# A two-layer decoder trunk in float32 split products: the expert loop takes two experts per turn, with one gather of 256 columns for both

## The chip, the cores and the metric

One core of a Trainium2 chip runs the whole program in one launch. The metric is the device time of an execution in microseconds (us). The profile is of one execution, taken by the hardware profiler; its engines are PE (TensorE; PEld are its weight loads), DVE (VectorE), ACT (ScalarE), POOL (GpSimd) and SP (SyncE, which issues the transfers).

## The reference, cut to what matters

256 tokens of width 1024 go through two layers. Each has an attention and convolution part (not touched by the change), and then a channel mixer: dense in layer 0, top-2-of-8 experts in layer 1.

```python
def swiglu(h, w1, w3, w2):
    return (jax.nn.silu(h @ w1) * (h @ w3)) @ w2

def moe_swiglu(h, router, w1, w3, w2):
    logits = (h @ router).astype(jnp.float32)
    top_vals, top_idx = lax.top_k(logits, TOP_K)
    top_w = jax.nn.softmax(top_vals, axis=-1)
    combine = jnp.sum(jax.nn.one_hot(top_idx, N_EXPERTS) * top_w[..., None], axis=-2)
    y = jnp.zeros(h.shape, jnp.float32)
    for e in range(N_EXPERTS):
        y = y + combine[..., e:e + 1] * swiglu(h, w1[e], w3[e], w2[e])
    return y
```

w1 and w3 of an expert are 1024 x 3584, w2 is 3584 x 1024, all float32, so the eight experts hold 352 MB, read once each.

## The kernel before, in words

**Split products.** Weights come in pieces of 1 MB (128 x 2048 float32) into a ring of 7 (`raw(t)`, `RAW`). For each piece ACT casts the high part to fp32r (`high_part`, L458), DVE subtracts it to get the low part (`low_part`, L686), and PE multiplies three times: high x high, high x low, low x high (12 matmuls of 512 columns a piece in `up`, L1320 to L1322, and in `down`, L1342 to L1344). There are 3 pairs of buffers for split pieces (`SPLIT`), so ACT may cast piece t only when PE is through with piece t - 3 (`w_used`). SP issues piece t + 7 when the low part of piece t is made.

**The expert loop.** A turn `j` is one expert and one pass over at most 128 of its tokens; a count on the device sets the number of turns, 8 with these inputs. Each turn has 42 pieces (`XS`), in the order of `expert_stream`: for each of 7 chunks c (`FCH`, 512 of the 3584 columns), two pieces of w1 (e1), two of w3 (e3), and, one chunk late, two of w2 (e2). Piece 40 and piece 41 are the two of e2 of the last chunk, 6. In this text e3(6) is the product of chunk 6 with w3, and down(5) the one with e2 of chunk 5.

For each chunk PE makes `up("e1", c)` into bank 0 or 1 and `up("e3", c)` into bank 2 or 3; ACT takes silu of the first into `sg` (L625); DVE multiplies by the second into `act` (L1008); PE transposes that, four 128 x 128 blocks into bank 4 (`transposes`, L1330); ACT and DVE split the result into `actT_hi` (L610) and `actT_lo` (L990); then `down(c)` adds it up in banks 5 and 6. There is one buffer each of `actT_hi` and `actT_lo`.

**Gather and scatter.** The tokens of an expert are picked by a product with a 0/1 matrix `sel` (tokens x 128 slots), which DVE makes by comparing positions (`select`, L944; L945 makes a float32 copy `sel_f`, which PE transposes to `selT` in the turn). A gather is four calls of `gather(q, b)`: 8 matmuls of 128 columns each (L1282), two calls with the high part of the tokens and two with the low part, 32 matmuls a turn. ACT copies the first two into `xe_hi` (L589), DVE the other two into `xe_lo` (L950). The result of a turn is scaled by the slots' weight (L597, L966), and 8 matmuls (`scatter`, L1300, L1301) and four additions (L681) put it back, early in the next turn.

**The order around the end of a turn** is written by hand, in each engine's own queue:

- PE: ..., e3(6), three gather calls for the next turn (L1365 to L1367), down(5), wait for `xe_hi`, the fourth gather call (L1379), transposes of chunk 6 (L1380), down(6) (L1381); then the next turn's e1(0).
- ACT: silu of chunk 6, high parts 39, 40 and 41, the two copies into `xe_hi` (L633), the high half of the transposed chunk 6 (L634), then high part 0 of the next turn. An activation table is loaded twice a turn, before the first cast (L458) and before the first silu (L625).
- DVE: low part 38, the low half of transposed chunk 5, low part 39, the product `act` of chunk 6 (L1008), low parts 40 and 41, the low half of transposed chunk 6 (L1018), the two copies into `xe_lo` (L1019), then the next turn.

Ahead of the loop stands one gather of its own (L1288 to L1292), with which the first turn starts.

Of the kernel before, what the change touches and what calls it, by code (L numbers as in the profile page):

```python
# [17 lines left out]
def hymba_trunk(nc, x, w_in, cmp_k_w1, cmp_v_w1, w_out, dense_w1, dense_w3, dense_w2,  # L18
# [27 lines left out]
    FB = BANK // P  # L46
    assert NT == 2 and NH == 2 and S <= 512 and FE % BANK == 0 and FD % P == 0 and L == 2
# [38 lines left out]
    assert XS % RAW == 0 and XS % SPLIT == 0 and BASE % SPLIT == 0  # L86

    ctx = ExitStack()
    with ctx:
# [12 lines left out]
        mixT = sb("mixT", [P, KD, S])  # L102
# [27 lines left out]
        pos_tab = sb("pos_tab", [P, NT, PASSES * E + 1])  # L130
# [13 lines left out]
        ARENA = 11944  # L144
        arena = attention_phase.enter_context(nc.sbuf_tensor("arena", [P, ARENA], F32))

# [41 lines left out]
        def sb_e(name, shape, dt=F32):  # L188
# [6 lines left out]
        sel = sb_e("sel", [P, NT, CAP], F32R)  # L195
        selT = sb_e("selT", [P, S], F32R)
        sel_f = sb_e("sel_f", [P, NT, CAP])
# [47 lines left out]
        sel_ready, self_ready, selT_psum, selT_ready = (  # L245
            sem("sel_ready"), sem("self_ready"), sem("selT_psum"), sem("selT_ready"))
# [50 lines left out]
        def wait_raw(eng, t, j=0):  # L297

            eng.wait_ge(piece_arrived[t % RAW], 16 * (t // RAW + 1) + j * (16 * XS // RAW))
# [15 lines left out]
        BACK = (3, 5, 6, 7)  # L315

# [4 lines left out]
        def _(sp):  # L321
# [40 lines left out]
            trips = sp.value_load(trips_i[0:1, 0:1], min_val=E, max_val=PASSES * E)  # L362
            with sp.If(trips > E):
                with sp.Fori(E, PASSES * E) as j:
                    stream_expert(j, j - E, False)
# [69 lines left out]
        def _(sc):  # L435
# [17 lines left out]
            def high_part(t, j=0):  # L453

                wait_raw(sc, t, j)
                if t >= SPLIT:
                    sc.wait_ge(w_used, j * XS + (t - SPLIT + 1))
                nc.scalar.copy(w_hi[t % SPLIT][:], raw(t)).then_inc(w_hi_ready, 1)  # L458
# [126 lines left out]
            def gathered_high(count):  # L585

                for h in range(2):
                    sc.wait_ge(xe_psum, count + h + 1)
                    nc.scalar.copy(xe_hi[:, 4 * h:4 * h + 4, :], bank[1 + 2 * h][:].rearrange("p (k s) -> p k s", k=4)) \  # L589
                        .then_inc(xe_hi_ready, 1)  # L590

            def scaled_high(j):

                sc.wait_ge(w_used, j * XS + BASE)
                sc.wait_ge(selT_ready, (j + 1) * 2)
# [4 lines left out]
            gathered_high(0)  # L600
            sc.wait_ge(trips_ready, 1)
            trips = sc.value_load(trips_i[0:1, 0:1], min_val=E, max_val=PASSES * E)
            with sc.Fori(0, trips) as j:
                def used(kind, c, half=1):

                    sc.wait_ge(w_used, j * XS + (BASE + xplace[kind, c, half] + 1))

                def actT_high(c):
                    sc.wait_ge(actT_psum, j * FCH + c + 1)
                    nc.scalar.copy(actT_hi[:], bank[4][:]).then_inc(actT_hi_ready, 1)  # L610

                done = 0
                for c in range(FCH):
                    e1_end = xplace["e1", c, 1]
                    while done <= min(e1_end + SPLIT, XS - 1):
                        high_part(BASE + done, j)
                        done += 1
                        if done == xplace["e3", 0, 0] + 1:
                            scaled_high(j)
                    if c >= 1:  # L620
                        actT_high(c - 1)
                    used("e1", c)
                    if c >= 2:
                        sc.wait_ge(act_ready, j * FCH + c - 1)
                    nc.scalar.activation(sg[:, c % 2, :], bank[c % 2][:], ACT.Silu).then_inc(sg_ready, 1)  # L625
                    if c == 3:
                        sc.wait_ge(selT_psum, j + 1)
                        nc.scalar.copy(selT[:], bank[7][:, 0:S]).then_inc(selT_ready, 1)
                        nc.scalar.copy(slot_weight[:], bank[7][:, S:S + 1]).then_inc(selT_ready, 1)
# [5 lines left out]
            scaled_high(trips)  # L635


        @block.vector
        def _(dv):
# [43 lines left out]
            def low_part(t, j=0):  # L683

                dv.wait_ge(w_hi_ready, j * XS + (t + 1))
# [249 lines left out]
            link(V.tensor_scalar(mcount[:, 0:1], mcount[:, 0:1], float(CAP), float(E), ALU.is_gt, ALU.mult))  # L935
            link(V.tensor_scalar(mcount[:, 0:1], mcount[:, 0:1], float(E), None, ALU.add))
# [3 lines left out]
            def select(j):  # L940

                for i in range(NT):
                    where = pos_tab[:, i, bass.ds(j, 1)]
                    V.tensor_scalar(sel[:, i, :], iota_f[:], where, None, ALU.is_equal).then_inc(sel_ready, 1)  # L944
                    V.tensor_scalar(sel_f[:, i, :], iota_f[:], where, None, ALU.is_equal).then_inc(self_ready, 1)  # L945

            def gathered_low(count):
                for h in range(2):
                    dv.wait_ge(xe_psum, count + 3 + h)
                    V.tensor_copy(xe_lo[:, 4 * h:4 * h + 4, :],  # L950
                                  bank[7 - 6 * h][:].rearrange("p (k s) -> p k s", k=4)).then_inc(xe_lo_ready, 1)
# [9 lines left out]
            def scaled_low(j):  # L961

                dv.wait_ge(selT_ready, (j + 1) * 2)
                for n in range(NH):
                    dv.wait_ge(ye_hi_ready, j * NH + n + 1)
# [5 lines left out]
            def add_back(j):  # L971

                for q, b in enumerate(BACK):
                    i, n = divmod(q, 2)
                    dv.wait_ge(back_psum, j * 4 + q + 1)
# [5 lines left out]
            gathered_low(0)  # L981
            trips = dv.value_load(trips_i[0:1, 0:1], min_val=E, max_val=PASSES * E)
            with dv.Fori(0, trips) as j:
                def used(kind, c, half=1):

                    dv.wait_ge(w_used, j * XS + (BASE + xplace[kind, c, half] + 1))

                def actT_low(c):
                    dv.wait_ge(actT_hi_ready, j * FCH + c + 1)
                    V.tensor_tensor(actT_lo[:], bank[4][:], actT_hi[:].bitcast(F32), ALU.subtract) \  # L990
                        .then_inc(actT_ready, 1)

                done = 0
                for c in range(FCH):
                    e1_end = xplace["e1", c, 1]
                    while done <= min(e1_end + SPLIT, XS - 1):
                        low_part(BASE + done, j)
                        done += 1
                        if done == xplace["e3", 0, 0] + 1:
# [440 lines left out]
```

## Time and profile before

| | us |
|---|---|
| three executions, lowest / median / highest | 1693.12 / 1693.9 / 1695.55 |
| the profiled execution, its own time | 1694.68 |
| its span, first to last instruction | 1692.7 |
| PE busy in the span | 1573.9 |
| DVE busy | 1223.2 |
| ACT busy | 912.5 |

The expert loop runs from 671 us to the end, some 60% of the span. A time of the profile counts from the first instruction of the span; "idle before" is how long the engine had nothing to do before the instruction, and behind `<-` stands what ended that.

### The profile page before, as it was taken

To read this page: it belongs to the slowest core of one execution; us is meant where nothing else is said; L and a number is where in the kernel's file an instruction comes from. 1 tells how busy PE (TensorE), PEld (TensorE's weight loads), DVE (VectorE), ACT (ScalarE), POOL (GpSimd) and SP (SyncE) were. 2 spreads that over 40 slices of the span, in tenths; PEclk is the share of its full clock that TensorE was granted. 3 is DMA by queue.
4 is the path that set the end of the run, shared out by engine and by line. 5 is a ranking of instruction groups with operands and counts; after the bars stand their busy time and mean duration, and the time that the engine had idled before them with its cause. 6 is when DMAs were issued, how large, how long until landed. Compare 5 with 4: busy or idle time off the path is not lost.

```text
span 1692.7 us, 19694 instructions
## 1 busy us (share of the span) xinstructions
PE 1573.9 (93%) x7276; PEld 1237.9 (73%) x7276; DVE 1223.2 (72%) x1210; ACT 912.5 (54%) x818; POOL 21.6 (1%) x37
## 2 busy tenths in 40 slices
PE   6978879998897886999999999999999999999997
PEld 5544369998754436888888888888888888888886
DVE  2866244443486625888988988988988988897886
ACT  1014233432111423777777777777777777777774
POOL 1010000000001000000000000000000000000000
PEclk9977889999897795999999999999999999999999
DMA  6510086542362003999999999999999998998992
GB/s 235 176 50 1 0 282 194 195 150 74 125 203 73 1 27 136 338 364 339 354 358 340 354 358 337 351 364 337 355 358 338 341 372 330 363 362 314 348 372 97
DMA packets 199355, 425.91 MB, mean 252 GB/s; under 512 B 7314, under 2 KB 40338, under 8 KB 199316
## 3 DMA queue, kind: packets, MB, share of 16 engines
q1 hardware_dynamic: 198000, 424.89, 69.6%
q10 hardware_dynamic: 1316, 0.49, 0.1%
q8 instruction: 25, 0.41, 0.1%
q14 instruction: 14, 0.11, 0.0%
HBM read 424.31 MB, written 1.05 MB: 251 GB/s over the span
## 4 chain that ended last, share of the span: by engine, by line
PE 84%; DVE 8%; issue 4%; ACT 3%; DMA 1%; POOL 0%; DVEq 0%; SPq 0%; POOLq 0%; ACTq 0%
PE bank L1320 11%; PE bank L1322 10%; PE bank L1321 10%; PE bank L1045 8%; PE bank L1342 6%; PE bank L1344 6%; PE bank L1343 6%; PE bank L1227 3%; PE bank L1229 3%; PE bank L1228 3%; PE bank L1208 2%; PE bank L1282 2%; PE bank L1167 2%; PE bank L1085 2%; DVE w_lo L686 1%
## 5 line engine op out<-in xcount | busy, mean ns | idle before, releaser
L686 DVE TENSOR_TENSOR w_lo<-ring,w_hi 128x2048 fp32r<-128x2048 f32 x369 | 842.2, 2290 | 191.3 <-ACT w_hi L458 190.0
L458 ACT CAST w_hi<-ring 128x2048 fp32r<-128x2048 f32 x369 | 704.8, 1913 | 294.7 <-PE bank L1322 159.0
L1320 PE MATMUL bank<-w_hi,xe_hi 128*128 128x512 f32 x896 | 355.2, 396 | 4.5 <-DVE w_lo L686 3.9
L1322 PE MATMUL bank<-w_hi,xe_lo 128*128 128x512 f32 x896 | 350.3, 391 | 0.0
L1321 PE MATMUL bank<-w_lo,xe_hi 128*128 128x512 f32 x896 | 349.8, 390 | 0.0
L1320 PEld LDWEIGHTS bank<-w_hi,xe_hi 128*128 128x128 f32 x896 | 168.8, 188 | 41.8 <-DVE w_lo L686 8.1
L1322 PEld LDWEIGHTS bank<-w_hi,xe_lo 128*128 128x128 f32 x896 | 168.6, 188 | 35.9
L1321 PEld LDWEIGHTS bank<-w_lo,xe_hi 128*128 128x128 f32 x896 | 168.9, 188 | 33.1
L1342 PE MATMUL bank<-w_hi,actT_hi 128*128 128x512 f32 x448 | 176.4, 394 | 11.8 <-DVE actT_lo L990 11.8
L1344 PE MATMUL bank<-w_hi,actT_lo 128*128 128x512 f32 x448 | 175.2, 391 | 0.0
L1343 PE MATMUL bank<-w_lo,actT_hi 128*128 128x512 f32 x448 | 175.1, 391 | 0.0
L1342 PEld LDWEIGHTS bank<-w_hi,actT_hi 128*128 128x128 f32 x448 | 84.5, 189 | 30.8 <-issue 13.7
L1227 PE MATMUL bank<-hT_hi,w_hi 128*128 128x256 f32 x352 | 100.7, 286 | 6.2 <-DVE w_lo L686 6.2
L1228 PE MATMUL bank<-hT_lo,w_hi 128*128 128x256 f32 x352 | 100.6, 286 | 0.0
L1229 PE MATMUL bank<-hT_hi,w_lo 128*128 128x256 f32 x352 | 100.6, 286 | 0.0
L1344 PEld LDWEIGHTS bank<-w_hi,actT_lo 128*128 128x128 f32 x448 | 84.5, 189 | 18.0
L1343 PEld LDWEIGHTS bank<-w_lo,actT_hi 128*128 128x128 f32 x448 | 84.4, 188 | 17.2
L710 DVE SCALAR_TENSOR_TENSOR arena<-arena,par 128x256 f32<-128x256 f32 x240 | 96.0, 477 | 0.0
L681 DVE TENSOR_TENSOR x_sb<-x_sb,bank 128x512 f32<-128x512 f32 x48 | 30.4, 682 | 68.4 <-PE bank L1208 59.7
L1227 PEld LDWEIGHTS bank<-hT_hi,w_hi 128*128 128x128 f32 x352 | 68.4, 194 | 6.7 <-issue 6.4
L1045 PE MATMUL bank<-ring,hT 128*128 128x512 f32 (+1 forms) x192 | 70.4, 528 | 0.0
L1228 PEld LDWEIGHTS bank<-hT_lo,w_hi 128*128 128x128 f32 x352 | 68.4, 194 | 0.4
(218 smaller groups left out, 1494.3 us busy)
## 6 DMA issues: line engine op xcount, KB each, us to landing
ring<-in_moe_w SPq DMA_DIRECT2D x336, 1024.0 KB, 6.4
ring<-in_dense_w SPq DMA_DIRECT2D x33, 1024.0 KB, 5.4
ring<-in_w_in SPq DMA_DIRECT2D x8, 2048.0 KB, 14.5
ring<-in_w_out SPq DMA_DIRECT2D x4, 2048.0 KB, 7.7
ring<-in_cmp_k_w SPq DMA_DIRECT2D x2, 2048.0 KB, 11.6
ring<-in_cmp_v_w SPq DMA_DIRECT2D x2, 2048.0 KB, 8.4
ring<-in_w_in SPq DMA_DIRECT2D x2, 1120.0 KB, 5.4
x_sb<-in_x SPq DMA_DIRECT2D x2, 512.0 KB, 4.7
```

What stands on the lines that cost most here:

```text
L458: nc.scalar.copy(w_hi[t % SPLIT][:], raw(t)).then_inc(w_hi_ready, 1)
L686: V.tensor_tensor(w_lo[t % SPLIT][:], raw(t), w_hi[t % SPLIT][:].bitcast(F32), ALU.subtract).then_inc(w_lo_ready, 1)
L1045: last = T.matmul(dst, lhs(k), rhs(k), start=(n == 0), stop=(n == len(chunks) - 1))
L1227: T.matmul(dst, hi[:, k, c], hT_hi[:, k, :], start=(k == 0), stop=False)
L1228: T.matmul(dst, hi[:, k, c], hT_lo[:, k, :], start=False, stop=False)
L1229: last = T.matmul(dst, lo[:, k, c], hT_hi[:, k, :], start=False, stop=(k == KD - 1))
L1320: T.matmul(dst, xe_hi[:, kk, :], hi[:, k, :], start=(kk == 0), stop=False)
L1321: T.matmul(dst, xe_hi[:, kk, :], lo[:, k, :], start=False, stop=False)
L1322: last = T.matmul(dst, xe_lo[:, kk, :], hi[:, k, :], start=False, stop=(kk == KD - 1))
L1342: T.matmul(dst, actT_hi[:, f], hi[:, k, r], start=first, stop=False)
L1343: T.matmul(dst, actT_hi[:, f], lo[:, k, r], start=False, stop=False)
L1344: last = T.matmul(dst, actT_lo[:, f], hi[:, k, r], start=False, stop=end)
```

## The change

A turn of the loop, now called `pair`, handles two experts, `h` = 0 and 1, whose bodies are written out one after the other; the number of turns is halved on the device. `sel`, `xe_hi` and `xe_lo` hold 256 columns, 128 for each expert; one gather of 8 calls with 4 matmuls of 256 columns each serves both, and stands at the end of the second expert. `sel_f` is gone (PE transposes `sel` itself). `actT_hi` and `actT_lo` have two buffers. The transposes of chunk 6 stand between the halves of down(5), and ACT and DVE split them ahead of pieces 40 and 41. ACT has a one-column silu at the start of each turn. Room for this comes from `mixT`, which now shares its place with tensors of the later stages. `nth(j, each, n)` computes the counts that are waited for. What follows is the core of it.

```diff
-        xe_hi, xe_lo = sb_e("xe_hi", [P, KD, CAP], F32R), sb_e("xe_lo", [P, KD, CAP], F32R)
-        actT_hi, actT_lo = sb_e("actT_hi", [P, BANK], F32R), sb_e("actT_lo", [P, BANK], F32R)
+        xe_hi = sb_e("xe_hi", [P, KD, PAIR * CAP], F32R)
+        xe_lo = sb_e("xe_lo", [P, KD, PAIR * CAP], F32R)
+        actT_hi, actT_lo = sb_e("actT_hi", [P, 2, BANK], F32R), sb_e("actT_lo", [P, 2, BANK], F32R)
...
+        QB = KD // 2
+        XE_BANK = (1, 3, 7, 0, 2, 1, 3, 7)
+        XE_AFTER = {5: 1, 6: 2, 7: 3}
...
(ACT)
+            def gathered_high(pair, q):
+                sc.wait_ge(xe_psum, pair * (2 * QB) + (q + 1))
+                nc.scalar.copy(xe_hi[:, 2 * q:2 * q + 2, :],
+                               bank[XE_BANK[q]][:].rearrange("p (k s) -> p k s", k=2)).then_inc(xe_hi_ready, 1)
...
+            with sc.Fori(0, pairs) as pair:
+                nc.scalar.activation(cstat[:, 1:2], ones[:, 0:1], ACT.Silu)
+                for h in range(PAIR):
...
-                while done < XS:
-                    high_part(BASE + done, j)
-                    done += 1
-                gathered_high(j * 4 + 4)
-                actT_high(FCH - 1)
+                    if h == PAIR - 1:
+                        for q in range(QB - 1):
+                            gathered_high(pair + 1, q)
+                    while done < xplace["e2", FCH - 1, 0]:
+                        high_part(BASE + done, j)
+                        done += 1
+                    actT_high(FCH - 1)
+                    while done < XS:
+                        high_part(BASE + done, j)
+                        done += 1
+                    if h == PAIR - 1:
+                        gathered_high(pair + 1, QB - 1)
...
(DVE)
-                while done < XS:
-                    low_part(BASE + done, j)
-                    done += 1
-                actT_low(FCH - 1)
-                gathered_low(j * 4 + 4)
+                        if c == 3 and h == PAIR - 1:
+                            dv.wait_ge(selT_psum, nth(j, 1, 1))
+                            select(pair + 1)
+                    while done < xplace["e2", FCH - 1, 0]:
+                        low_part(BASE + done, j)
+                        done += 1
+                    actT_low(FCH - 1)
+                    while done < XS:
+                        low_part(BASE + done, j)
+                        done += 1
+                    if h == PAIR - 1:
+                        for q in range(QB):
+                            gathered_low(pair + 1, q)
...
(PE)
+            def gather(q):
+                src, b = (h_hi, h_lo)[q // QB], XE_BANK[q]
+                for k in range(2):
+                    kk = 2 * (q % QB) + k
                     for i in range(NT):
-                        last = T.matmul(bank[b][:, k * CAP:(k + 1) * CAP], src[:, i, kk * P:(kk + 1) * P],
+                        last = T.matmul(bank[b][:, k * S:(k + 1) * S], src[:, i, kk * P:(kk + 1) * P],
                                         sel[:, i, :], start=(i == 0), stop=(i == NT - 1))
                 last.then_inc(xe_psum, 1)
...
+                        if c == FCH - 1 and h == PAIR - 1:
+                            pe.wait_ge(sel_ready, pair * (NT * PAIR) + 2 * NT * PAIR)
+                            pe.wait_ge(act_ready, nth(j, FCH, FCH - 1))
+                            pe.wait_ge(selT_ready, nth(j, 2, 4))
+                            gather(0)
+                            gather(1)
+                            gather(2)
+                        down(c - 1, 0)
+                        if c == FCH - 1:
+                            transposes(c)
+                        down(c - 1, 1)
...
-                pe.wait_ge(xe_hi_ready, j * 2 + 3)
-                gather(3, 1)
-                transposes(FCH - 1)
-                down(FCH - 1)
+                    if h == PAIR - 1:
+                        for q in range(3, 2 * QB):
+                            if q in XE_AFTER:
+                                pe.wait_ge(xe_hi_ready, pair * QB + (QB + XE_AFTER[q]))
+                            gather(q)
+                    down(FCH - 1, 0)
+                    down(FCH - 1, 1)
```

## Rows read from the trace of the kernel before

**Rows 1.** The page: the span, and PE's busy time and its share.

```profile
span 1692.7 us, 19694 instructions
PE 1573.9 (93%) x7276; PEld 1237.9 (73%) x7276; DVE 1223.2 (72%) x1210; ACT 912.5 (54%) x818; POOL 21.6 (1%) x37
```

**Rows 2.** Busy time by stage, one turn a row; behind it PE clock, DMA share, GB/s.

```profile
1171.50:1297.40 125.90, 124.35 (x579) 102.98 (x579) 109.39 (x69) 92.18 (x65) 0.00 (x0) 1.00 0.95 350
...
1423.20:1549.10 125.90, 124.31 (x579) 102.96 (x579) 109.40 (x69) 92.15 (x65) 0.00 (x0) 1.00 0.96 350
1549.10:1676.60 127.50, 125.93 (x579) 104.08 (x579) 109.37 (x69) 91.25 (x64) 0.00 (x0) 0.99 0.81 296
```

**Rows 3.** The waits in the expert loop, longest in total first.

```profile
ACT w_hi L458 <- PE bank L1322: 159.0, 193, 3.2
DVE w_lo L686 <- ACT w_hi L458: 129.8, 224, 3.1
...
PE bank L1342 <- DVE actT_lo L990: 11.8, 8, 1.5
```

**Rows 4.** Timeline of PE near the end of a turn: start, duration, instruction.

```profile
1154.43 0.60 PE L1330 MATMUL bank<-ident,hn 128*128 128x128 f32 x4
1154.78 0.48 PE L1320 MATMUL bank<-w_hi,xe_hi 128*128 128x512 f32 x1
...
1160.34 1.90 PE L1282 MATMUL bank<-sel,h_hi 128*128 128x128 f32 x16
1162.07 1.06 PE L1282 MATMUL bank<-sel,h_lo 128*128 128x128 f32 x8
1162.96 0.45 PE L1342 MATMUL bank<-w_hi,actT_hi 128*128 128x512 f32 x1
...
1168.52 1.03 PE L1282 MATMUL bank<-sel,h_lo 128*128 128x128 f32 x8
1169.39 0.62 PE L1330 MATMUL bank<-ident,hn 128*128 128x128 f32 x4
1171.49 0.49 PE L1342 MATMUL bank<-w_hi,actT_hi 128*128 128x512 f32 x1 [1.48 <-DVE actT_lo L990]
```

**Rows 5.** Timeline of ACT near the end of the same turn.

```profile
1157.82 1.92 ACT L458 CAST w_hi<-ring 128x2048 fp32r<-128x2048 f32 x1 [0.30 <-PE bank L1322]
1160.54 1.91 ACT L458 CAST w_hi<-ring 128x2048 fp32r<-128x2048 f32 x1 [0.80 <-PE bank L1322]
...
1167.81 1.06 ACT L589 CAST xe_hi<-bank 128x512 fp32r<-128x512 f32 x2
1170.05 0.58 ACT L610 CAST actT_hi<-bank 128x512 fp32r<-128x512 f32 x1 [1.18 <-PE bank L1330]
1170.65 1.28 ACT L458 ACT_TABLE_LOAD   x1
```

**Rows 6.** Timeline of DVE near the end of the same turn.

```profile
1159.76 2.29 DVE L686 TENSOR_TENSOR w_lo<-ring,w_hi 128x2048 fp32r<-128x2048 f32 x1 [0.30 <-ACT w_hi L458]
1161.97 0.68 DVE L1008 TENSOR_TENSOR hn<-hn,bank 128x512 f32<-128x512 f32 x1
...
1170.66 0.69 DVE L990 TENSOR_TENSOR actT_lo<-bank,actT_hi 128x512 fp32r<-128x512 f32 x1 [0.43 <-ACT actT_hi L610]
1171.27 1.28 DVE L950 CAST xe_lo<-bank 128x512 fp32r<-128x512 f32 x2
```

**Rows 7.** Timeline of PE in the dense stage: matmuls of 256 columns, and one behind.

```profile
339.76 0.28 PE L1227 MATMUL bank<-hT_hi,w_hi 128*128 128x256 f32 x1
...
340.48 0.40 PE L1243 MATMUL bank<-w_hi,dact_hi 128*128 128x512 f32 x1
```

**Rows 8.** Timeline of the entry into the loop: the first gather, and the first matmul.

```profile
660.53 3.65 PE L1282 MATMUL bank<-sel,h_hi 128*128 128x128 f32 x16 [5.04 <-DVE h_lo L958]
663.98 3.62 PE L1282 MATMUL bank<-sel,h_lo 128*128 128x128 f32 x16
...
671.45 0.79 PE L1320 MATMUL bank<-w_hi,xe_hi 128*128 128x512 f32 x1 [3.85 <-DVE w_lo L686]
```

**Rows 9.** Clock and rates of one short stretch, PE alone; columns as in rows 2.

```profile
1549.30:1552.70 3.40, 3.40 (x9) 0.50 0.81 298
```

**Rows 10.** DMA queues from 655 to 800 us: rates in 40 slices, and the instruction queue.

```profile
GB/s 0 5 0 0 21 388 394 246 379 293 115 401 354 322 362 397 405 402 381 388 377 412 331 301 346 363 371 326 388 392 402 410 407 386 388 388 360 294 225 76
...
q8 instruction: 5, 0.08, 0.2%
```

More of the change, by code:

```diff
@@ L46, in hymba_trunk @@
     FB = BANK // P
+    PAIR = 2
     assert NT == 2 and NH == 2 and S <= 512 and FE % BANK == 0 and FD % P == 0 and L == 2
@@ L598, in scaled_high @@
                                          scale=slot_weight[:, 0:1]).then_inc(ye_hi_ready, 1)
-            gathered_high(0)
+            for q in range(QB):
+                gathered_high(0, q)
             sc.wait_ge(trips_ready, 1)
[L602 to L615, printed above, removed]
+            pairs = sc.value_load(trips_i[0:1, 0:1], min_val=E // PAIR, max_val=PASSES * E // PAIR)
@@ L980, in _ @@
             V.memset(mcount[:, 0:1], 0.0).then_inc(added, 1)
[L981 to L996, printed above, removed]
+            for q in range(QB):
+                gathered_low(0, q)
@@ new lines, in _, with split_piece, up, transposes @@
+            pairs = pe.value_load(trips_i[0:1, 0:1], min_val=E // PAIR, max_val=PASSES * E // PAIR)
+            with pe.Fori(0, pairs) as pair:
+                for h in range(PAIR):
+                    j = pair, h
+                    own = slice(h * CAP, (h + 1) * CAP)
+                    def split_piece(kind, c, half, k):
+                        t = BASE + xplace[kind, c, half]
+                        pe.wait_ge(w_lo_ready, nth(j, XS, t + 1))
+                        return split_views(t, k)
+                    def up(kind, c):
+                        dst = bank[(0 if kind == "e1" else 2) + c % 2][:]
+                        if kind == "e1" and c >= 2:
+                            pe.wait_ge(act_ready, nth(j, FCH, c - 1))
+                        for half in range(2):
+                            hi, lo = split_piece(kind, c, half, 4)
+                            for k in range(4):
+                                kk = 4 * half + k
+                                T.matmul(dst, xe_hi[:, kk, own], hi[:, k, :], start=(kk == 0), stop=False)
+                                T.matmul(dst, xe_hi[:, kk, own], lo[:, k, :], start=False, stop=False)
+                                last = T.matmul(dst, xe_lo[:, kk, own], hi[:, k, :], start=False, stop=(kk == KD - 1))
+                            last.then_inc(w_used, 1)
+                    def transposes(c):
+                        pe.wait_ge(act_ready, nth(j, FCH, c + 1))
+                        if c >= 1:
+                            pe.wait_ge(actT_ready, nth(j, FCH, c))
+                        for k in range(FB):
+                            last = T.transpose(bank[4][:, k * P:(k + 1) * P], act[:, c % 2, k * P:(k + 1) * P],
+                                               ident[:])
+                        last.then_inc(actT_psum, 1)
+                    def down(c, half):
+                        pe.wait_ge(actT_ready, nth(j, FCH, c + 1))
@@ L1341, in down @@
                                 dst, r = bank[5 + n][:], slice(n * BANK, (n + 1) * BANK)
-                                T.matmul(dst, actT_hi[:, f], hi[:, k, r], start=first, stop=False)
-                                T.matmul(dst, actT_hi[:, f], lo[:, k, r], start=False, stop=False)
-                                last = T.matmul(dst, actT_lo[:, f], hi[:, k, r], start=False, stop=end)
+                                T.matmul(dst, actT_hi[:, c % 2, f], hi[:, k, r], start=first, stop=False)
@@ new lines, in _ @@
+                    scatter(j)
+                    for c in range(1, FCH):
+                        up("e1", c)
+                        transposes(c - 1)
+                        if c == 1:
+                            pe.wait_ge(added, nth(j, 4, 2))
+                        up("e3", c)
+                        if c == 1:
+                            pe.wait_ge(added, nth(j, 4, 5))
+                        if c == FCH - 1 and h == PAIR - 1:
[9 more added lines that the diff above has]
+                        down(c - 1, 1)
+                        if c == 2:
+                            pe.wait_ge(sel_ready, pair * (NT * PAIR) + NT * PAIR)
+                            for i in range(NT):
+                                T.transpose(bank[7][:, i * P:(i + 1) * P], sel[:, i, own].bitcast(F32), ident[:])
+                            for i in range(NT):
+                                last = T.matmul(bank[7][:, S:S + 1], sel[:, i, own].bitcast(F32),
+                                                wgt_tab[:, i, bass.ds(pair * PAIR + h, 1)],
+                                                start=(i == 0), stop=(i == NT - 1))
+                            last.then_inc(selT_psum, 1)
```

241 lines of the change are left out of this document (103 added, 138 removed).

## The prediction

> **What bounds the kernel now.** First the page: PE is busy 93% of the span, DVE 72%, ACT 54% [rows 1]. Such shares are means, so next comes the loop alone, a turn at a time: a turn takes 125.9 us and PE is busy 124.35 of them, DVE 109.4, ACT 92.2; the weights arrive at 350 GB/s [rows 2]. Then the waits: PE waits once a turn, 1.5 us for the low half of the transposed last chunk, 8 times, 11.8 us in all; ACT and DVE do most of the waiting, ACT for PE to release a buffer and DVE for ACT [rows 3]. So PE's own queue sets the time, and a matmul that goes is worth its whole length. But DVE, at 109.4 of 125.9, has only 16.5 us a turn to spare, and everything that PE eats passes through ACT and then DVE with three buffers between. What must be read from the timelines is therefore what these two queues do at the turn's end.
>
> **Gathers.** Before, a turn has 24 gather matmuls in 2.62 us (1160.34 to 1162.96) and 8 in 0.87 (1168.52 to 1169.39), 109 ns each, 3.49 a turn and 6.98 for two experts [rows 4]. After, it is 32 matmuls of 256 columns for both. The dense stage has such matmuls, six in 0.72 us, 120 ns each [rows 7]: 3.84 us. Twice the columns for 10% more time: **-3.14 us for a pair**. The copies out of the banks are as many per pair as before, 512 columns each.
>
> **The old wait.** From the start of the last transposes to the next matmul it is 2.10 us (1169.39 to 1171.49); elsewhere in the turn the same four transposes take 0.35 (1154.43 to 1154.78) [rows 4]. So the wait costs 1.75 us, and both of a pair go: **-3.50 us**. Were nothing late in its place, the pair would gain 6.64 us.
>
> **What is late next, first expert of a pair.** I lay out the queues from the moment T at which PE is through with e3(6); before, that is 1160.34 [rows 4]. A piece takes PE 2.72 us, the distance of two casts in step with it (1157.82, 1160.54) [rows 5]. The transposes now stand between the halves of down(5), so they run from T + 2.72; the product they need is ready at T + 2.3 (1161.97 + 0.68) [rows 6]. The second half ends at T + 2.72 + 0.35 + 0.12 + 2.72 = T + 5.9 (0.12 for the change of kind of matmul). Then PE wants low part 40. Before, ACT cast it ahead of everything, at T + 0.2 (1160.54) [rows 5]. Now the cast stands behind the high half of the transposed chunk, which waits for the transposes: it starts 0.66 us after they do (1169.39 to 1170.05) and takes 0.58, to T + 3.96; the cast of 40 runs to T + 5.8; DVE subtracts for 2.29, to T + 8.15; PE goes on at T + 8.2 [rows 4 to 6]. **A wait of 2.3 us takes the place of 1.75.** The half product that was to cover the transposes covers them, but the piece behind is now late.
>
> **Second expert.** Here ACT's queue has three of the new copies into `xe_hi` ahead of cast 39. They wait for PE's gather calls, which begin only at T. Before, cast 39 began at T - 2.52 (1157.82) and its low part at T - 0.58 (1159.76) [rows 5, 6]. Now: gather calls 0 to 2, 12 matmuls, T to T + 1.44; the third copy starts at about T + 1.75 and takes 0.58; cast 39 ends at T + 4.15; low part 39 at T + 6.5; only then, behind it in DVE's queue, the product of chunk 6, to T + 7.1; PE's transposes at T + 7.2. PE has been idle since the first half of down(5), T + 1.44 + 0.12 + 2.72 = T + 4.3. **A wait of 2.9 us** for L1008. Then transposes and second half to T + 10.4, the five gather calls left (20 matmuls, 2.4 us) to T + 12.8, down(6) to T + 18.35. Meanwhile ACT: high half to T + 8.4, casts 40 and 41 to T + 12.1, last copy, table load 1.28, cast 0 of the next pair to T + 15.7. DVE: low part 40 to T + 12.6, 41 to T + 14.8, then four copies into `xe_lo` at 0.6 each (two took 1.28 [rows 6]) to T + 17.1, low part 0 to T + 19.3. **PE waits 1.0 us** at the start of the next pair.
>
> **The small parts.** ACT loads a table once in a pair instead of four times, 1.28 us each [rows 5], and DVE makes 4 comparisons instead of 8. Neither is waited for: PE's only wait is the one above [rows 3], so I count nothing; if their cover were gone, PE would already be waiting elsewhere. `sel_f` and `mixT` cost nothing in time. The transfers: 88 MB in 251.4 us is 350 GB/s as before, and slices of the first turn reach over 400 [rows 10].
>
> **Entry and end.** At the entry the clock is low: 16 gather matmuls take 3.45 us (660.53 to 663.98) [rows 8]. With 256 columns at half clock I estimate 0.24 each: 3.84 for 16, 7.7 for all. The last copies into `xe_lo` end some 0.8 us later, the silu of one column adds under 0.2 beside them: **+0.8 us** before the first matmul at 671.45. After the last pair no next expert follows, so the 1.0 us wait is paid three times, not four.
>
> **Sum.** A pair: -3.14 - 3.50 + 2.3 + 2.9 + 1.0 = -0.44. Four: -1.8; last wait not paid: -1.0; entry +0.8: **-2.0 us**.
>
> **The clock.** Of the eight waits of 1.5 us one, at 1549, was followed by a fall of the granted clock to 0.50 (1.2 GHz instead of 2.4) for 3.4 us [rows 9]; that turn took 127.5 us instead of 125.9, so a fall costs 1.6 us [rows 2]. After there are four waits of 2.9 us with transposes next to them, and four of 2.3. Each is longer than the one that fell. Bounds: no fall (-1.6 us against before) and all eight (7 more, +11.2). I take the end nearer to the row, one wait in eight, and since waits are longer, one fall more than before: +1.6 us.
>
> -2.0 + 1.6 = -0.4. The profiled execution, 1694.68 us, would be 1694.3; it stands 0.8 above the median of three, so the median comes to **1693.5 us**. With no fall it is 1690.3, with four falls 1696.7. About 0.2%, 3.4 us, is what a measurement of this kernel can tell from no change.
>
> **Rivals.**
> - *The waits eat the gain* (the forecast), 0.53, at 1693.5. For it: both new delays follow from the order of each queue and durations that the trace has. Against: each is a difference of long chains, and an error of 0.6 us a pair moves it by 2.4.
> - *The design works*: ACT and DVE are far enough ahead. Full: 4 x -6.64 + 0.8 = -25.8, 1668 us. Partial: only the wait for L1008 is absent (the copies into `xe_hi` don't hold up cast 39 so long), 4 x -2.9, 1682. Together 0.19, 0.07 for the full one. For it: ACT is busy only 92 of 125.9 us. Against: what holds ACT is its order, not its load.
> - *The clock falls after every long wait*: its place is the two ends of an expert, its price 1.6 us each, and it decides from about four falls. Eight: -2.0 + 11.2 = +9.2, **1703 us**, slower. 0.18. For it: every new wait is longer than the one after which the clock fell. Against: seven of eight didn't fall.
> - *The loop body no longer stays on the chip.* Before, a turn shows 579 matmuls and as many weight loads [rows 2]; the instruction queue moved 5 packets of 16 KB in the first turn [rows 10]. After, the body is twice as long, and if it must be loaded again at each branch back, PE's queue can run dry there. Bound below: nothing, since the engine waits there anyway; above: the largest idle time at a first entry, 3.85 us [rows 8], three times less the 1.0 us waits: +8.6, 1702. 0.10, with 1698 as its middle. The Trainium skill, Runtime: NRT & Kernel Launch, section Instruction fetch mechanics, gives PE room for 2048 instructions and says that a taken branch to a page that isn't there waits for its fetch. By that rule the doubled body, some 2,300 matmuls and loads, would not fit where 1,158 did; that the old one is loaded once the queue's rows agree with, and how long a fetch at the branch takes no row shows.
>
> **How the numbers follow.** Below 1690.5 lie the design case (0.19) and the low end of the forecast (0.09): faster 0.28. Within: 0.38 of the forecast, 0.03 of the clock case, 0.06 of the code case: 0.47. Slower: 0.06 + 0.15 + 0.04 = 0.25. The range leaves out the design case, 0.19, and goes from the forecast with error and few falls, 1687, to all waits falling, 1703. The forecast's own range is 1689 to 1698.
>
> **What would show it.** Right: PE waits for DVE L1008 near 2.9 us four times, for low part 40 near 2.3 us four times, for low part 0 near 1 us three times; gather matmuls 120 ns apart; a pair every 251 us; one table load a pair; ACT's copies into `xe_hi` waiting over 3 us for the gather; DVE still at some 218 us a pair. Wrong: a pair under 249 us, or waits on `w_lo` in other places, which would mean that the transfers or DVE bind; falls of the clock at more than four waits move it to the third case; idle of PE at the branch with weights ready, to the fourth.

## The result, and the profile after

The changed kernel takes **1705.9 us** (median of four, 1703.3 to 1710.9) against 1694.6 for the kernel before: ratio 1.0071, interval 1.0046 to 1.0096. It is slower, by 11 us, where no clear change was forecast, and it lies above the range of the prediction. The profiled execution is the longest of the four, 1710.92 us, span 1709.2. Of the 16.5 us between this span and that of the kernel before (1692.7), 3.9 us arise ahead of the first gather (it starts at 664.4 us instead of 660.5), in stages whose work the change does not touch, and 13.4 in the loop. From the first gather to the loop's first matmul it is 0.5 us less.

First the page of the changed kernel: span, busy times, the instruction queue, and that queue's row on the page of the kernel before. Line numbers are those of the changed kernel.

```profile
span 1709.2 us, 19381 instructions
...
PE 1573.7 (92%) x7148; PEld 1233.7 (72%) x7148; DVE 1222.2 (72%) x1196; ACT 898.1 (53%) x812; POOL 21.6 (1%) x37
...
q8 instruction: 63, 1.03, 0.2%
```

```profile
q8 instruction: 25, 0.41, 0.1%
```

PE has 128 matmuls less (the gathers) and is as long busy as before [rows 1]: something stretched the others. ACT is 14 us less busy: three of the four table loads of a pair are gone, and nobody is faster for it. The instruction queue moved 63 packets in the whole execution, against 25 before; of the 25 five fell in the first turn [rows 10] and none after 800 us.

Now the loop, one pair of experts a row (columns as in [rows 2], where two turns are 251.8 us):

```profile
794.00:1050.70 256.70, 249.66 (x1125) 205.91 (x1125) 218.15 (x133) 180.46 (x127) 0.00 (x0) 0.98 0.94 344
1050.70:1306.20 255.50, 248.19 (x1125) 204.75 (x1125) 218.15 (x133) 180.44 (x127) 0.00 (x0) 0.99 0.95 345
1306.20:1564.70 258.50, 250.92 (x1125) 206.83 (x1125) 218.12 (x133) 180.38 (x127) 0.00 (x0) 0.97 0.94 341
```

A pair takes 3.7 to 6.7 us more than two old turns, not 0.4 less. DVE works 218 us in it, as forecast. The clock, 1.00 before in turns without a fall, is 0.97 to 0.99.

What PE waits for in the loop (total, times, longest) answers to [rows 3]:

```profile
PE bank L1364 <- DVE hn L1033: 10.7, 4, 2.7
PE bank L1376 <- DVE w_lo L707: 8.2, 4, 2.1
PE bank L1354 <- DVE w_lo L707: 4.9, 2, 2.6
PE bank L1354 <- issue: 2.8, 1, 2.8
```

L1364 are the last transposes, which wait for the product of chunk 6 in the second expert; L1376 is down(6) in the first expert, for low part 40; L1354 is the first matmul of the next pair. The first two were forecast at 2.9 and 2.3 us and are 2.68 and 2.06. The third was forecast at 1.0 and is 2.3, 2.57 and 2.84.

The timelines show that the first two arise as laid out. Second expert, PE, ACT and DVE around T = 910.02, the start of the gather (start, duration, instruction):

```profile
910.02 1.60 PE L1312 MATMUL bank<-sel,h_hi 128*128 128x256 f32 x12
911.46 0.40 PE L1376 MATMUL bank<-w_hi,actT_hi 128*128 128x512 f32 x1
...
917.04 0.66 PE L1364 MATMUL bank<-ident,hn 128*128 128x128 f32 x4 [2.68 <-DVE hn L1033]
```

```profile
910.70 1.56 ACT L598 CAST xe_hi<-bank 128x512 fp32r<-128x512 f32 x3 [3.50 <-PE bank L1312]
912.14 1.93 ACT L468 CAST w_hi<-ring 128x2048 fp32r<-128x2048 f32 x1
```

```profile
914.10 2.29 DVE L707 TENSOR_TENSOR w_lo<-ring,w_hi 128x2048 fp32r<-128x2048 f32 x1 [4.95 <-ACT w_hi L468]
916.31 0.68 DVE L1033 TENSOR_TENSOR hn<-hn,bank 128x512 f32<-128x512 f32 x1
```

Twelve gather matmuls take 1.44 us, 120 ns each. ACT is idle for 3.50 us with cast 39 behind its three copies; DVE is idle 4.95 us; the product ends at T + 7.0 (forecast 7.1) and PE goes on at T + 7.0 (7.2).

What was not forecast is what the clock does behind these waits. Stretches of 6 us from the end of each of the eight waits, PE alone (busy, then granted clock):

```profile
794.00:800.00 6.00, 5.99 (x19) 0.72 0.78 268
917.00:923.00 6.00, 5.96 (x26) 0.72 0.55 179
1050.70:1056.70 6.00, 6.00 (x19) 0.72 0.82 273
1173.70:1179.70 6.00, 5.96 (x26) 0.72 0.53 175
1306.20:1312.20 6.00, 6.00 (x19) 0.72 0.80 268
1429.20:1435.20 6.00, 6.00 (x26) 0.72 0.53 175
1564.70:1570.70 6.00, 6.00 (x26) 1.00 0.79 269
1686.10:1692.10 6.00, 5.97 (x26) 0.72 0.01 3
```

Seven of eight show 0.72, that is 3.4 us at 0.50 (1.2 GHz) and the rest at 2.4 GHz. At two of the three branches back the clock is down too, for one such length and for two, so the profile has ten such lengths in the loop, against one before [rows 9].

Last, the branch back itself, in PE's sequencer: changed kernel, then kernel before (minimum, median, maximum in ns).

```profile
L1335 PEldq COMPARE_BRANCH  x4: 83/6171/6591, 925.8 to 1694.9; - x4
```

```profile
L1305 PEldq COMPARE_BRANCH  x8: 76/208/244, 795.4 to 1678.2; - x8
```

The last branch falls through. The three that go back take 6.0 to 6.6 us instead of 0.2. The first is reached at 925.8 while PE has work until 929.9; it ends at 931.8, and PE goes on at 932.2. The low part that the waits name was ready at 929.3, 0.6 us before PE ran out: DVE's row is

```profile
926.96 4.49 DVE L707 TENSOR_TENSOR w_lo<-ring,w_hi 128x2048 fp32r<-128x2048 f32 x2
```

and the first of the two operations in it takes 2.29 us. So it is the branch that ends this wait, though the waits put it down to `w_lo`.

The time between the loop's first matmul and the start of its last scatter splits into three terms. A fall of the clock costs 1.62 us here (the long turn of [rows 2] less a normal one, before rounding); "waits" is PE's idle stretches over 0.6 us.

| profiled execution | loop | lengths of low clock | waits | remainder |
|---|---|---|---|---|
| before | 1013.2 | 1: 1.6 | 11.8 | 999.8 |
| changed | 1026.6 | 10: 16.2 | 26.7 | 983.7 |
| difference | +13.4 | +14.6 | +14.9 | -16.1 |

(The 2.4 us that PE waits just before the last scatter, in every kernel here, are in the remainder. So is the low clock with which the loop is entered, 4.1 us of it before and 4.6 after.)

### The profile page after: what moved, and what is told of

The parts are those of the page before. It is cut to its first block, busy times and chain, and to the rows that moved or that the text cites. A ratio compares the mean times of both kernels' runs of the same rounds, so it can differ in the third digit from the quotient of the medians.

```text
span 1709.2 us, 19381 instructions
## 1 busy us (share of the span) xinstructions
PE 1573.7 (92%) x7148; PEld 1233.7 (72%) x7148; DVE 1222.2 (72%) x1196; ACT 898.1 (53%) x812; POOL 21.6 (1%) x37
## 4 chain that ended last, share of the span: by engine, by line
PE 86%; DVE 7%; issue 3%; ACT 2%; DMA 1%; POOL 0%; SPq 0%; ACTq 0%; DVEq 0%; POOLq 0%
PE bank L1354 12%; PE bank L1356 12%; PE bank L1355 12%; PE bank L1075 8%; PE bank L1376 5%; PE bank L1377 5%; PE bank L1378 5%; PE bank L1257 3%; PE bank L1258 3%; PE bank L1259 2%; PE bank L1238 2%; PE bank L1197 2%; DVE w_lo L707 2%; PE bank L1115 2%; ACT w_hi L468 2%
## 5 line engine op out<-in xcount | busy, mean ns | idle before, releaser
L1354 PE MATMUL bank<-w_hi,xe_hi 128*128 128x512 f32 x896 | 357.6, 399 | 11.9 <-DVE w_lo L707 9.1
L1354 PEld LDWEIGHTS bank<-w_hi,xe_hi 128*128 128x128 f32 x896 | 169.9, 190 | 47.8 <-DVE w_lo L707 10.8
L1376 PE MATMUL bank<-w_hi,actT_hi 128*128 128x512 f32 x448 | 180.3, 402 | 8.2 <-DVE w_lo L707 8.2
L1377 PE MATMUL bank<-w_lo,actT_hi 128*128 128x512 f32 x448 | 179.0, 400 | 0.0
L1376 PEld LDWEIGHTS bank<-w_hi,actT_hi 128*128 128x128 f32 x448 | 86.6, 193 | 27.8 <-DVE w_lo L707 9.9
```

Of the source, the lines that this page charges most:

```text
L1354: T.matmul(dst, xe_hi[:, kk, own], hi[:, k, :], start=(kk == 0), stop=False)
L1376: T.matmul(dst, actT_hi[:, c % 2, f], hi[:, k, r], start=first, stop=False)
L1377: T.matmul(dst, actT_hi[:, c % 2, f], lo[:, k, r], start=False, stop=False)
```

## The experiments

Theory A: two of PE's new waits come from the order of ACT's and DVE's queues. Theory B: what costs most is the clock, which falls behind them. Theory C: PE's code in the loop is loaded again at each branch back. Rivals: the gather or the transfers set the pair; the clock and the code have no part. All runs of one group of four stood beside the same kernel before, 1694.5 and 1693.9 us.

### The order of ACT's queue in the second expert: e1_cast39_first

```diff
-                    if h == PAIR - 1:
-                        for q in range(QB - 1):
-                            gathered_high(pair + 1, q)
                     while done < xplace["e2", FCH - 1, 0]:
                         high_part(BASE + done, j)
                         done += 1
+                    if h == PAIR - 1:
+                        for q in range(QB - 1):
+                            gathered_high(pair + 1, q)
```

> The changed kernel with one edit: ACT makes the high part 39 ahead of its first three copies into xe_hi, not behind them. The changed kernel took 1705.9 us. Theory A (the order of ACT's queue makes PE wait for L1008): the four waits of PE for L1008, 2.68 us each, go, the four for low part 40, 2.06 us, stay; -10.7 us for the waits and, if a fall of the clock of 1.6 us goes with each (theory B), some 5 to 6 more: 1690 us with B, 1695 without. Rival: ACT and DVE are late for another reason and the wait only moves to low part 39 or to L1015: over 1703 us. Theory C (the branch back takes 6 us because PE's code is loaded again) says nothing of this run but that the branch still takes over 5 us three times.

**1681.2 us**, 0.9916 [0.9899, 0.9933] of the kernel before: 25 us less than the changed kernel, more than expected. What PE waits for in the loop:

```profile
PE bank L1376 <- DVE w_lo L707: 8.2, 4, 2.1
PE bank L1354 <- DVE w_lo L707: 5.0, 3, 1.9
```

The waits for L1033 (L1008 before) are gone, the four of 2.06 us stay to the hundredth. Of the 25.0 us between the two profiled loops 10.7 are these waits, 2.7 are shorter waits behind the branch, and 11.3 are seven lengths of low clock less (3 instead of 10). The rival falls. The branch back takes 4.5 to 5.0 us, a little less than the over 5 that was expected.

### The first expert alone: e8_cast40_first

```diff
-                    while done < xplace["e2", FCH - 1, 0]:
+                    while done <= xplace["e2", FCH - 1, 0]:
```

(in ACT's and in DVE's queue; the copies into `xe_hi` stay ahead of cast 39)

> The changed kernel with part 40 made ahead of the halves of the transposed last chunk, but with ACT's three copies into xe_hi still ahead of high part 39. Theory A: the four waits of 2.06 us in the first expert of a pair go, the four of 2.68 us for L1008 in the second stay: 1705.9 - 8.2 for the waits, and with theory B some 3 to 4 falls less, 5 to 6 us: 1692 us. If the parts add up, e1_cast39_first and this one together give e2_casts_first. Rival (the first expert's end costs nothing, all comes from the second): 1704 us.

**1680.0 us**, 0.9920 [0.9903, 0.9937]; 12 us better than expected. PE's waits:

```profile
PE bank L1364 <- DVE hn L1033: 10.7, 4, 2.7
PE bank L1354 <- issue: 3.0, 3, 1.3
```

8.2 us of waits go, and so do all but two lengths of low clock. Two of the four 2.68 us waits have a fall behind them here, and two of the four of 2.06 us in e1; in the changed kernel it was seven of eight. So whether the clock falls is not a matter of the wait's length alone: a wait of the same length does and does not bring it.

### Both: e2_casts_first

(ACT casts 39 and 40 ahead of the copies into `xe_hi` and of the split, DVE makes low part 40 ahead of the split)

> As e1_cast39_first, and in both experts ACT makes the high part 40, and DVE the low part 40, ahead of the halves of the transposed last chunk. Theory A: both waits go, in the first expert of a pair (2.06 us, 4 times) as in the second (2.68 us, 4 times), 19 us in all. With theory B the falls of the clock behind them go too, 7 were seen behind these 8 waits in the profile of the changed kernel, 1.6 us each: 1705.9 - 19 - 9 = 1678 us; without B 1687. With theory C three waits of 2.3 to 2.8 us stay at the start of a pair. Rival (the gather or the transfers set the pair): over 1695 us, with waits for w_lo elsewhere.

**1665.5 us**, 0.9836 [0.9810, 0.9862]: 40 us less than the changed kernel and **29 us less than the kernel before**. All of PE's waits in the loop and at its end:

```profile
PE bank L1354 <- issue: 3.9, 3, 1.4
PE bank L1330 <- DVE ye_lo L987: 2.4, 1, 2.4
```

No wait at an expert's end, no fall of the clock in the loop. It went 12 us under what was expected; 3.8 of that are shorter waits behind the branch (3.9 in place of 7.7), 4.9 the three lengths of low clock there, and some 2 that seven lengths were counted at 9 us and cost 11.3; the rest is not assigned. The two edits don't add up: each alone takes 25 us off, both together 40, since seven or eight of the ten lengths of low clock go with either one.

### PE kept busy where it sat idle: e7_filled_waits

This one leaves every order as it is in the changed kernel, and puts matmuls whose result nobody reads into the gaps at the experts' ends.

```diff
+                    def fill(count):
+                        pe.wait_ge(sg_ready, nth(j, FCH, FCH))
+                        for _ in range(count):
+                            T.matmul(bank[0][:], h_hi[:, 0, 0:P], h_hi[:, 0, 0:BANK], start=True, stop=True)
...
                         down(c - 1, 0)
                         if c == FCH - 1:
+                            if h == 1:
+                                fill(11)
                             transposes(c)
                         down(c - 1, 1)
+                        if c == FCH - 1 and h == 0:
+                            fill(9)
```

> The changed kernel with matmuls of 512 columns that nobody reads put where PE sat idle: 9 before down(6) of the first expert of a pair (2.04 us in place of the 2.06 us wait), 11 before the last transposes of the second (2.49 us in place of 2.68). No wait is removed and no other order changes; PE is only kept busy. Theory B (each of these waits is followed by a fall of the granted clock, 7 of 8 in the profile, 1.6 us each): the falls behind them go, 1705.9 - 7 x 1.6 = 1694.7 us, 1691 to 1698, and the granted clock stays at 1.00 around the ends of the experts. Rival (the clock has no part; the lost time is the waits and the reload of code): 1705.9 us or more, within 3.

**1692.6 us** (ten runs, 1689.1 to 1696.7), 0.9989 [0.9976, 1.0001]: 13 us less than the changed kernel by doing 80 matmuls more. The same eight places, stretches of 6 us that begin some 0.5 us before the filled gap ends:

```profile
788.80:794.80 6.00, 5.98 (x26) 1.00 0.76 265
910.10:916.10 6.00, 5.82 (x37) 1.00 0.54 176
1042.10:1048.10 6.00, 5.98 (x27) 1.00 0.75 256
1163.40:1169.40 6.00, 5.82 (x37) 1.00 0.51 175
1293.30:1299.30 6.00, 5.97 (x26) 1.00 0.73 252
1414.60:1420.60 6.00, 5.82 (x37) 1.00 0.50 175
1546.50:1552.50 6.00, 5.98 (x26) 1.00 0.69 246
1667.80:1673.80 6.00, 5.82 (x37) 1.00 0.00 0
```

1.00 in all eight. This is the run that shows theory B: the gaps are there, 18 us of them, only filled; what is gone is the low clock behind them. Of the 14.6 us between the two profiled loops 13.0 are eight lengths of low clock less and 2.3 shorter waits at the branch; the filled gaps cost 0.7 more than the empty ones. The two falls that are left are at the branch back.

The run also shows what the wait for low part 0 is when the clock holds. PE's last matmul of the first pair, its next one, and DVE's low parts from 0 on:

```profile
921.54 0.39 PE L1383 MATMUL bank<-w_hi,actT_lo 128*128 128x512 f32 x1
923.91 0.79 PE L1354 MATMUL bank<-w_hi,xe_hi 128*128 128x512 f32 x1 [1.99 <-issue]
```

```profile
920.59 6.68 DVE L707 TENSOR_TENSOR w_lo<-ring,w_hi 128x2048 fp32r<-128x2048 f32 x3
```

Low part 0 is ready at 922.9, 0.95 us after PE ran out at 921.9; the branch ends at 923.5, later still.

### The code doubled, nothing else: e3_two_turns

```diff
-            with pe.Fori(0, trips) as j:
+            with pe.Fori(0, trips) as pair:
+                for turn in range(2):
+                    j = Turn(pair, turn)
```

(so on ACT and DVE too; `Turn` turns `j * n + m` into counts of `pair`, and the number of turns is halved)

> The kernel before with nothing changed but that a turn of the loop is two of the old turns written out one after the other: every gather of 128 columns, every order and every buffer as before. PE's code in the loop doubles. Theory C: the instruction queue moves some 60 packets instead of 25, the branch takes 6 us instead of 0.2 at three of the four turns' ends, PE waits 2 to 3 us behind it, and with falls of the clock the time is 1694.6 + 7 to 12: 1702 to 1706 us. Rival (the wait at a pair's start in the changed kernel is for low part 0, as forecast, and code has no part in it): 1694.6 us within 2.

**1694.1 us** (ten runs), 0.9997 [0.9987, 1.0007]: the same as before, where theory C asked for 1702 to 1706. Yet the code is loaded again: 63 packets of the instruction queue as in the changed kernel, and the branch:

```profile
L1331 PEldq COMPARE_BRANCH  x4: 83/3892/3907, 921.0 to 1677.3; - x4
```

PE's waits:

```profile
PE bank L1371 <- DVE actT_lo L1016: 11.8, 8, 1.5
...
PE bank L1349 <- issue: 0.4, 2, 0.2
```

The branch takes 3.9 us instead of 0.2, and PE's queue holds 4.1 us of work when it is reached. PE goes on 0.4 us behind the branch's end, so 0.2 us shows. Reloading is real and by itself costs next to nothing. With the gather for two and the new tail the branch takes longer: 4.1 to 5.2 us in e1, e2, e7 and e8, and waits of 0.4 to 2.0 us show. In the changed kernel, 6.0 to 6.6 and 2.3 to 2.8.

What makes the difference stands in the traces. PE and the transfers during the first branch back of e4, e3, e2, e7 and the changed kernel (behind the clock the DMA share and GB/s):

```profile
915.90:919.30 3.40, 3.40 (x17) 1.00 0.03 10
921.00:924.90 3.90, 3.90 (x19) 1.00 0.40 155
912.10:917.20 5.10, 4.09 (x19) 1.00 0.70 232
918.50:923.50 5.00, 3.42 (x16) 1.00 0.98 366
925.80:931.80 6.00, 4.09 (x19) 1.00 0.92 310
```

In each of the 21 branches back of these seven kernels one packet of the instruction queue, 16 KB, starts while the branch lasts. It starts 1.0 us after the branch is reached in e4, 1.4 to 1.5 in e3, 1.7 to 2.7 in e1, e2, e7 and e8, and 3.5 to 4.3 in the changed kernel; it takes 0.9 to 1.3 us; and the branch ends 1.3 to 1.6 us behind the packet's end in every one. So what differs is how late the packet comes. It comes soonest where hardly any weights move (e4); the rate alone does not order the others, since e7 moves more than the changed kernel and waits less.

### The gather for two experts alone: e4_old_tail

```diff
                         down(c - 1, 0)
-                        if c == FCH - 1:
-                            transposes(c)
                         down(c - 1, 1)
...
                     if h == PAIR - 1:
+                        pe.wait_ge(act_ready, nth(j, FCH, FCH))
                         for q in range(3, 2 * QB):
...
+                    transposes(FCH - 1)
                     down(FCH - 1, 0)
```

(ACT and DVE make parts 40 and 41 first, then copy into `xe_hi` and split the transposes, as in the kernel before)

> The changed kernel with the second part undone: the transposes of the last chunk stand behind down(5) and behind the gather again, ACT and DVE make parts 40 and 41 before they split them, and ACT's copies into xe_hi stand behind part 41. The gather of 256 columns for two experts and the two experts written out stay. Theory A: per pair 1.75 us of wait twice in place of 2.06 + 2.68, so about 4 us less in waits and with shorter waits fewer falls of the clock (theory B): 1705.9 - 4 - 5 = 1697 us, still above the kernel before less the 12.6 us of gathers, because of the branch (theory C). Rival (the tail is what gains and the gather what costs): over 1706 us.

**1678.1 us**, 0.9910 [0.9886, 0.9933], 19 us better than expected. Against e3, which differs by the gather for two with what belongs to it (its copies and comparisons, the room made by `mixT`, the one-column silu), that is -16.0 us. Of the difference between the two profiled executions the loop makes 14.4 us, with waits 1.5 us longer; without waits and falls it is 15.8, or 4.0 for a pair. The change's first part is a clear gain. PE's waits are as long as before or little longer (13.3 us in 8), with one fall behind them.

### The new tail alone: e5_tail_alone, and with the casts first: e6_tail_casts_first

The kernel before with two buffers of the transposes' halves and

```diff
-                    down(c - 1)
+                    down(c - 1, (0,))
+                    if c == FCH - 1:
+                        transposes(c)
+                    down(c - 1, (1,))
```

> The kernel before with the second part of the change alone: two buffers of actT_hi and actT_lo, the last transposes between the halves of down(5), and ACT and DVE splitting them ahead of parts 40 and 41. One expert a turn, gathers of 128 columns. Theory A: in each of the 8 turns the wait of 1.48 us for the low half of the transposes gives way to one of about 2.06 us for low part 40, +4.6 us; with theory B falls behind about half of them, +5: 1699 to 1705 us. Rival (the half product covers the transposes and nothing is late behind): 1694.6 - 12 = 1683 us or less.

**1699.7 us**, 1.0038 [1.0023, 1.0052]: slower, at the lower end of what was expected. The place of the wait is another one than expected:

```profile
PE bank L1288 <- ACT xe_hi L589: 16.1, 8, 2.0
```

2.01 us in each turn, for the copy into `xe_hi` that the fourth gather call needs. That copy stands behind casts 40 and 41, and these now behind the split of the transposes. The mechanism is the one of theory A, the victim stands one call ahead of down(6).

(e6 is e5 with ACT's cast 40 and DVE's low part 40 ahead of the split)

> As e5_tail_alone, but ACT makes the high part 40 and DVE the low part 40 ahead of the halves of the transposed last chunk. Theory A: no wait at the end of a turn, 8 x 1.75 us less than the kernel before, and no fall of the clock behind one: 1694.6 - 14 - 1 = 1679.5 us. Against e2_casts_first (1665.5 us), which differs by the gather for two experts and by the reload of code, it should be 12 to 14 us slower, the gathers' 12.6 and little else. Rival (the transposes cost the same wherever they stand): over 1690 us.

**1682.5 us**, 0.9936 [0.9919, 0.9952], 3 us more than expected; it is 17 us slower than e2, where 12 to 14 were expected. PE's waits:

```profile
PE bank L1306 <- DVE ye_lo L969: 2.4, 1, 2.4
PE bank L1288 <- ACT xe_hi L589: 1.7, 8, 0.2
```

With part 40 moved the half product covers the transposes as it should, 0.2 us a turn excepted. So the second part of the change is worth -11 us with the right order behind it and +6 without.

All kernels, split in the same way (profiled executions, us; in e7 the remainder holds the 18.1 us of filling matmuls):

| | median | loop | lengths of low clock | waits | remainder |
|---|---|---|---|---|---|
| changed | 1705.9 | 1026.6 | 10 | 26.7 | 983.7 |
| e1 | 1681.2 | 1001.6 | 3 | 13.2 | 983.5 |
| e8 | 1680.0 | 999.7 | 2 | 13.3 | 983.1 |
| e2 | 1665.5 | 986.1 | 0 | 3.9 | 982.3 |
| e4 | 1678.1 | 998.8 | 1 | 13.3 | 983.9 |
| e7 | 1692.6 | 1012.0 | 2 | 5.4 | 985.2 + 18.1 |
| e3 | 1694.1 | 1013.2 | 1 | 11.8 | 999.7 |
| e5 | 1699.7 | 1017.8 | 1 | 16.1 | 1000.1 |
| e6 | 1682.5 | 1001.9 | 0 | 0 | 1001.9 |

The remainder is 982 to 985 for six kernels with the gather for two, and 1000 to 1002 for those without, whatever the waits and the clock did: the split holds, with an error of 1 to 2 us.

## Why the prediction was wrong

- **What bounds, and the gathers: right.** PE sets the time throughout. 256 columns take 120 ns. The gather part is worth 4.0 us a pair (remainders of e4 and e3), not 3.14. The gather matmuls themselves stand 109 ns apart in e3 and 120 in e4, as forecast; the rest of that difference is not assigned.
- **The two waits at an expert's end: right in place, measured 0.2 us shorter.** 2.68 for 2.9 and 2.06 for 2.3; e1 and e8 each take away the one that the order names and leave the other at the same hundredth, and e2 takes away both.
- **The wait at the pair's start: wrong cause, wrong size.** The step "PE waits 1.0 us" for low part 0 failed. DVE had that part ready at T + 19.2, as forecast (19.3). PE, forecast to run out at T + 18.35, ran out at T + 19.9: the fall of the clock behind the wait before had cost it 1.6 us. In e7, without that fall, the part is 0.95 us late, which is the forecast's 1.0. But in e7 the branch ends later still, and in the changed kernel PE stood still for the branch alone, 2.3 to 2.8 us. Of the sum's terms this one measured 7.7 us in place of 3.0. The fourth rival named the mechanism, and its bound (3.85 us a time) held. By the Trainium skill, Runtime: NRT & Kernel Launch, section Instruction fetch mechanics, PE has room for 2048 instructions. The instruction queue's rows agree: a loop of 1,158 matmuls and loads is loaded once (25 packets in the whole execution, none after 800 us), one of twice as many again in each turn (63). The same section says that a taken branch out of a window of two pages, 256 instructions each, waits for a fetch. The old loop is more than four such pages long, and its branches took 0.2 us with no packet after 800 us; there the measurement decides. That a fetch at a taken branch holds PE up is true in the changed kernel and almost hidden in e3.
- **The clock: this is the step that failed.** "One fall more than before" carried the share of the waits of 1.48 us, one in eight, over to longer waits, for which no row stood. Nine lengths more came, 14.6 us in place of 1.6: behind seven of the eight waits at the experts' ends, and three lengths at the branches. Length alone would not have told it either: behind the eight waits of 2.01 us in e5 the clock fell once. The third rival, all waits falling, 1703 us, was the nearest of the cases, and it stood at 0.18. e7 shows the term by itself: eight lengths, 13.0 us, between the same gaps empty and filled.
- **No change in sum: wrong.** Waits +14.9 (forecast +12.0: 2.3 and 2.9 four times, 1.0 three times, less 11.8), remainder -16.1 (forecast -14.8), entry -0.5 (forecast +0.8), clock +14.6 (forecast +1.6). Without the clock that is -1.7, next to the forecast's -2.0, and this nearness is in part luck: the branch's 4.7 us too much are made up for by shorter waits at the experts' ends (1.9), by the remainder and by the entry (1.3 each). The entry was priced at half clock throughout (0.50 before); in the changed kernel the mean clock there is 0.66. The range ended where the clock case ended and did not put the code case on top of it; both came together.

**Open:** what holds the instruction packet back among the weights. In e3 and e4 one piece of weights was in flight when the branch was reached, in e1, e7 and the changed kernel two; that was not tried by itself, and it does not tell the changed kernel (3.5 to 4.3 us) from e7 (2.1 to 2.6). Open is also why the same wait brings a fall of the clock in one place and not in another. How the 1705.9 of the median splits into falls is known for the profiled execution only; the mean granted clock is 0.936 in it and 0.937 to 0.939 in the three others, which will have had a little less low clock.

## What to carry to other kernels

Moving a step ahead on one engine is half a change: whatever stands in the other engines' queues behind the work that now waits for it moves too. Here cast 39 stood behind copies that waited for the gather, and part 40 behind the split that waited for the transposes, though neither needs them; putting both first turned +11 us into -29. And an idle gap of PE can cost more than its length: the waits of 2.06 us cost 2.06 where the clock held and 3.7 where it fell. Read the granted clock behind each gap before pricing it. A wait that the profile puts down to one engine can be another's: lay the end of the branch beside the end of the named work.

## What the runs showed of the hardware that was not expected

- Matmuls without use, placed in PE's gaps, made the kernel 13 us faster (1705.9 to 1692.6). The granted clock stayed at 1.00 behind them, which is 13.0 of the 14.6 us between the two profiled loops.
- The clock fell behind one of eight gaps of 1.48 us (before, and again in e3; none of four in e4), one of four of 1.85 (e4), one of eight of 2.01 (e5), two of four of 2.06 (e1), two of four of 2.68 (e8) and seven of the eight of 2.06 and 2.68 together (changed).
- A branch back to code that is loaded again takes 3.5 to 6.6 us in PE's sequencer instead of 0.2, and is nearly free as long as PE's queue holds that much work: 4.1 us of it in e3 and e4. It ends 1.3 to 1.6 us behind the end of one 16 KB packet of the instruction queue, which starts 1.0 us after the branch is reached with 10 GB/s of weights moving (e4), 2.6 us after with 366 (e7) and 3.5 us after with 310 (changed).
- Two of the four table loads of a pair are gone in e3, and ACT is busy for 181.9 us of a pair instead of 184.2, with the time unchanged: nobody waits for them.
